# A two-block transformer on one core: filler transposes while TensorE waits at norms, block seams and router

## The reference

```python
def hybrid_layer(...):                      # first block, twice
    h = rmsnorm(x, norm1_w) * (1 + sc1) + sh1
    u = h @ w_in                            # 1024 x 5632
    ...                                     # pooling, short convolution, attention
    x = x + g1 * (merged @ w_out)
    h2 = rmsnorm(x, norm2_w) * (1 + sc2) + sh2
    x = x + g2 * ((silu(h2 @ w_gate) * (h2 @ w_up)) @ w_down)

def second_block(...):
    h = layer_norm(x, ln_in_g, ln_in_b)
    for l in range(2):
        mix = mixer_sublayer(h, ...)        # h @ w_in, 16 attention heads, @ w_out
        h = layer_norm(ALPHA * h + mix, ln1_g[l], ln1_b[l])
        scores = sigmoid(h @ router_w)      # 16 experts
        # best group of 4 experts, then the best 2 of its experts
        for e in range(16):
            y += gate[:, e] * ((silu(h @ w_gate[e]) * (h @ w_up[e])) @ w_down[e])
        h = layer_norm(ALPHA * h + y, ln2_g[l], ln2_b[l])
    return h
```

## Time and profile before

| | us |
|---|---|
| median of 3 runs (lowest, highest) | 1684.8 (1683.87, 1691.77) |
| the profiled execution, its own time | 1684.51 |
| its span, first to last instruction | 1682.7 |
| PE busy | 1567.5 (93% of the span) |
| DVE busy | 930.2 (55%) |
| ACT busy | 624.3 (37%) |
| weights moved | 427.66 MB, mean 254 GB/s |
| mean granted clock of PE | 0.966 of full |

### The profile page before, as it was taken

The page is one execution under the profiler, slowest core; times in us unless marked ns, Lnnn a source line. Parts: engine busy times, 40 slices in busy tenths (PEclk is TensorE's granted clock), DMA queues, the critical chain, the costliest instruction groups (busy, mean ns, idle before and its releaser), DMA issues.

```text
span 1682.7 us, 19021 instructions
## 1 busy us (share of the span) xinstructions
PE 1567.5 (93%) x7519; PEld 1072.6 (64%) x7519; DVE 930.2 (55%) x1401; ACT 624.3 (37%) x904; POOL 49.8 (3%) x66
## 2 busy tenths in 40 slices
PE   2899998999899998999989998999988999999996
PEld 2777787888778787788878774333336876433332
DVE  5888687865578978755467864111006786211002
ACT  2354544434344464444335742111114573111111
POOL 2000000000000000000030200000000110000000
PEclk8899999999999999999989998999998998999998
DMA  9677555976567734765565337999995417799995
GB/s 340 220 249 245 185 177 179 318 259 225 190 232 256 271 126 152 274 209 176 190 162 188 101 128 302 410 409 409 409 371 176 153 51 267 305 409 408 409 409 215
DMA packets 149980, 427.66 MB, mean 254 GB/s; under 512 B 8120, under 2 KB 16560, under 8 KB 149888
## 3 DMA queue, kind: packets, MB, share of 16 engines
q1 hardware_dynamic: 146208, 417.43, 67.8%
q0 software_dynamic: 3456, 8.87, 1.8%
q10 hardware_dynamic: 224, 0.07, 0.0%
HBM read 425.30 MB, written 1.05 MB: 253 GB/s over the span
## 4 chain that ended last, share of the span: by engine, by line
PE 62%; DVE 17%; DMA 7%; SPq 7%; ACT 4%; issue 3%; DVEq 0%; ACTq 0%
PE gp L2341 26%; PE gp L2788 9%; PE gp L2564 9%; SPq L756 6%; PE gp L2807 4%; DVE wlo L1424 4%; DMA raw<-in_w_in 3%; PE mp L2828 2%; DMA raw_deep<-in_exp_w_up 2%; PE gp L2773 2%; ACT whi L872 2%; DMA raw_deep<-in_w_ada 2%; DVE acc L1296 1%; DVE ft L1485 1%; PE mp L2625 1%
## 5 line engine op out<-in xcount | busy, mean ns | idle before, releaser
L1424 DVE TENSOR_TENSOR wlo<-raw,whi 128x2048 fp32r<-128x2048 f32 (+1 forms) x131 | 287.2, 2193 | 171.0 <-ACT whi L872 168.8
L872 ACT ACTIVATE whi<-raw 128x2048 fp32r<-128x2048 f32 (+1 forms) x131 | 240.0, 1835 | 297.3 <-PE gp L2341 162.7
L2341 PE MATMUL gp<-whi,xt_hi 128*128 128x512 f32 (+1 forms) x792 | 313.9, 396 | 16.7 <-DVE xt_lo L1495 7.4
L2341 PE MATMUL gp<-whi,xt_lo 128*128 128x512 f32 (+1 forms) x792 | 305.0, 385 | 0.0
L2341 PE MATMUL gp<-wlo,xt_hi 128*128 128x512 f32 (+1 forms) x792 | 304.7, 385 | 0.0
L2341 PEld LDWEIGHTS gp<-whi,xt_hi 128*128 128x128 f32 x792 | 151.0, 191 | 54.7 <-issue 14.4
L2341 PEld LDWEIGHTS gp<-whi,xt_lo 128*128 128x128 f32 x792 | 150.7, 190 | 30.2
L2341 PEld LDWEIGHTS gp<-wlo,xt_hi 128*128 128x128 f32 x792 | 151.0, 191 | 27.6 <-issue 1.0
L2196 DVE TENSOR_SCALAR pr<-slots,key,dg 128x128 f32<-128x128 f32 x64 | 19.3, 343 | 255.2 <-PE gp L2818 255.2
L1296 DVE SCALAR_TENSOR_TENSOR acc<-raw,cact,acc 128x1024 f32<-128x1024 f32 x69 | 88.5, 1282 | 2.6 <-DMA raw<-in_w_ada 1.1
L2210 DVE TENSOR_TENSOR pr<-pr,gp 64x512 f32<-64x512 f32 x32 | 21.7, 679 | 123.3 <-ACT pr L1214 123.3
(11 more groups left out here) (443 smaller groups left out, 2476.1 us busy)
## 6 DMA issues: line engine op xcount, KB each, us to landing
raw<-in_w_in SPq DMA_DIRECT2D x60, 1024.0 KB, 5.8
raw<-in_w_ada SPq DMA_DIRECT2D x42, 1024.0 KB, 5.3
raw_deep<-in_exp_w_gate SPq DMA_DIRECT2D x28, 1024.0 KB, 16.2
raw_deep<-in_exp_w_up SPq DMA_DIRECT2D x28, 1024.0 KB, 14.9
raw_deep<-in_exp_w_down SPq DMA_DIRECT2D x28, 1024.0 KB, 15.0
raw<-in_w_gate SPq DMA_DIRECT2D x20, 1024.0 KB, 5.1
raw<-in_w_up SPq DMA_DIRECT2D x20, 1024.0 KB, 5.2
raw<-in_w_down SPq DMA_DIRECT2D x20, 1024.0 KB, 5.0
```

Source lines behind the costliest of these rows:

```text
L872: act.activation(halves1(s, l, units, cols)[0], slot(raw, g % RAW, units, cols), ACT.Copy).then_inc(hi_done.sem, 1)
L1424: dve.tensor_tensor(lo, slot(raw, g % RAW, units, cols), hi.bitcast(F32), ALU.subtract).then_inc(raw_read[g % RAW].sem, 1)
L2341: mm = pe.matmul(gp[:, q % 2, t, 0:wide], a[:, chunk, ts], w[:, unit, c0:c0 + wide], start=first and n == 0 and m == 0, stop=last and n == ...
```

## The change

A helper, `keep_busy(bank, n)`, transposes the 128x128 identity n times into the first 128 columns of a PSUM bank that nothing reads. It is called at six places, 192 such transposes in all: 28 behind `turn_tile(0)` in `begin` (three calls), 40 ahead of the turn of tile 0 in layer 1 of the second block, 10 behind that turn in both layers, 8 behind `folded(0)` in both routers, and 16 ahead of the first gather in both. Where the bank is one of a dense pair, a wait for `pair_free` stands ahead; the product behind it has the same wait.

```diff
+            def keep_busy(bank, n):
+
+                for _ in range(n):
+                    pe.transpose(bank[:, 0:P], ident[:, :], ident[:, :])
...
                     pe.wait_ge(*xn_ready.at(l, xn0 + 1))
                     turn_tile(0)
+                    q = group_jobs(s0)[0][0]
+
+                    pe.wait_ge(*pair_free[q % 2].at(l, 2 * (q // 2)))
+                    keep_busy(gp[:, q % 2, 0, :], 28)
                     pe.wait_ge(*ft_lo.at(l, f0 + 1))
                     product(s0, (0,))
...
+                if l > 0:
+                    keep_busy(bank_xg, 40)
                 turn_tile(0)
+
+                pe.wait_ge(*pair_free[0].at2(l, 0))
+                keep_busy(gp[:, 0, 0, :], 10)
                 for s in range(2):
                     pe.wait_ge(*ft_lo.at2(l, X2_IN + s + 1))
                     product(s, (0,))
...
                 logits(0)
                 folded(0)
+                keep_busy(bank_gu, 8)
 
                 pe.wait_ge(*x2_sum.at2(l, 5))
...
                     if c == 0:
+                        if group == 0:
+                            keep_busy(bank, 16)
                         pe.wait_ge(*pick_ready.at2(l, NT * (group + 1)))
```

## The result

The changed kernel took 1697.6 us (median of 20 runs, 1687.3 to 1704.2), the kernel before, on the same chip, 1690.5 (20 runs, 1680.8 to 1694.0). The ratio is 1.0041, with a 95% interval of 1.0028 to 1.0054: about 7 us slower, where 0.8 us was forecast, and outside the range. Half of the miss is in the base: the 1684.5 us of before's profiled execution is near the low end of its runs.

The account below looks back on a forecast made before the run. PE was taken as busy nearly throughout but partly at half clock, with each stretch set by its last-ending chain; 1684.51 - 2.2 (layer 1) + 3.0 (routers) = 1685.3, stated as 1685.5 us, range 1679.5 to 1691.

Parts of the forecast that it names:

- Second block, layer 1: Start of layer 1's second block: fillers keep the clock full, unit 2's product starts earlier, all passed on: 2.2 us faster.
- The three calls of `begin`: At each `begin`: fillers fit PE's idle time, but the chain runs over DVE and ACT, so 0 gained.
- The routers: Both routers: fillers stand where PE is wanted, each 1.5 us slower, +3.0 for both.
- The two terms: In each router: +1.0 for the 8 behind `folded(0)`, +0.5 for the 16 ahead of the gather.
- one to one: Expert stage: bound by loading, its stream without a hole, so a router's delay of 1.5 us shifts it in full.
- lower bound of -1.8 for both: Both routers' best case, each with a full clock throughout; the 16 came to -0.2 if the clock is held.
- the first rival: Routers' fillers cost nothing net, the clock full and the gather warm: -4.0 in all, 1680.5 us; chance 0.2.
- Second block, layer 0: Start of layer 0's second block: DVE's chain sets the time, ten fillers end ahead of `wlo`; 0 gained.
- The gain stands alone: Layer 1's -2.2 kept and routers' fillers costing nothing net, -1.8: 1680.5 us; chance 0.2.
- The transposes don't hold the clock: By the skill's rule no stretch is held; layer 1 loses 1.7, each router 5.3: 1697 us; chance 0.07.
- The rises that I had argued from: Two clock rises behind eight transposes and some 512-wide matmuls, one in layer 1, taken to show that transposes hold the clock.
- All cold time comes back: PE sets the time at every seam, so 25.3 us come back: 1659.5 us; chance 0.04.

Follow-up runs that it names:

- the delays of 1.5 and 2.0 us: Kernel before plus transposes ahead of layer 1's second-block attention: 14 with untouched seam, 1.0041; 18 with the ten fillers in each seam, 0.9991.
- the 20: Kernel before plus 20 fillers ahead of the fourth head's value product of the first block, in each layer: 0.9974, again 0.9979.
- e3_router: Kernel before plus only the routers' fillers, 8 and 16 in each layer: 1.0023, or +3.9 us.
- e7_fourteen: The whole change with 14 fillers in place of the 40, timed against the kernel before: 1.0068.
- the 14: 14 fillers in place of the 40: 1.0068 in the otherwise whole change; 1.0013 with the routers' 8 and 16 out, 5 ahead of the flag wait.
- e2_seam: Kernel before plus only the second block's fillers, 10 in layer 0, 40 and 10 in layer 1: 1.0035, or +5.9 us.
- e5_forty: Kernel before plus only the 40 fillers ahead of layer 1's second-block turn of tile 0: 1.0009.

## Why the prediction was wrong

- **The base.** The step "The profiled execution lies 0.3 below the median of before" took the times of three runs for the kernel's. In the comparison the median was 1690.5, 5.7 us above the 1684.8 that I used. The repeats of before had spans of 1689.1 and 1687.3.
- **Second block, layer 1: the step that failed.** It failed twice. "40 fillers are 4.4 us at the full clock, which PE still has when they start; they end a microsecond ahead of the turn": they start 2.1 us late behind "issue" idle time, the clock is at half for 3.5 us of them, and they overran the turn by 2.7 us (20.1 us from that last expert matmul to the turn before, 22.8 after). The rest of the sum was right, and due to the ten: the tens alone shortened the seam by 2.2 us. With both it gained 0.8 to 1.1. Then "so all of it is passed on: -2.2 us" failed, and this is what the time shows: with the seam 2.2 us shorter, the tens alone were 3.2 and 4.1 us slower by their two ratios. Attention 1 behind them took 140.7 and 140.6 us, 4.3 more than before, and 141.0 in two of three profiles of the changed kernel. I had priced everything behind the seam as merely shifted. That is true only while the clock stays the same there, and the delays of 1.5 and 2.0 us show that it doesn't.
- **The three calls of `begin`: 0.** Right at the places named: the chain at the first is unmoved, PE waits longer for L1424 (0.89 us against 0.64), the clock holds (in six profiles with the 28s it was full at 14 of 18 calls, in the others at none). The 28s alone gave 1.0004. Further on, the first block's stage is 208.8 to 210.9 us in six profiles with the 28s, mean 209.7, and 203.7 to 210.3 in eleven without them or the 20, mean 207.5; the clock was at half at the wait named next for 6.8 to 10.2 us in all of the six and for 0 to 6.8 in the eleven. The wait for L1632 in it, whose cold matmuls follow, was 1.1 to 2.7 us with, 0 to 2.4 without. That a sooner `begin` sends PE sooner into this wait would fit, but the two ranges overlap and no experiment isolates it.
- **The routers: +3.0.** The two terms were mis-sized, the sum was near: luck, since the errors cancel. Eight fillers took 1.74 us up to the next row, 1.8 forecast. But from the router's turn to the flag five profiles with them (two layers each) average 16.0 us and eleven without 16.3: -0.3, not +1.0, in each router (single ones lie between 15.0 and 17.3 either way). The sixteen: load averages 12.1 us with them and 11.2 without, +0.9, not +0.5. The expert stage, which I had as shifted "one to one", is 214.6 us on average with them and 213.9 without: +0.7 more, by the late fall of the clock in four of ten. Together 1.3 for each router, 2.6 for both; by the timed runs of `e3_router` +3.9 (0.8 to 7.1). The prediction's lower bound of -1.8 for both doesn't follow from its own -0.2 for each, and the first rival's sum rests on it.
- **Second block, layer 0: 0.** The tens add nothing to the seam there (turn to turn 9.35 us before and after). Attention 0 behind it is long or short in either kernel.
- **The rivals.** *The gain stands alone* needed free routers: they aren't. *The transposes don't hold the clock* comes near in time (1697) and is wrong in cause: in the changed kernel's first profile the clock is 1.00 through all three `begin`s. The rule of the Trainium skill (TensorE: Matmul & The Clock Gate, Part 4: PE-mode transpose), that the full clock does not engage for transposes, is not borne out by these fp32 transposes: 28 ran at 0.11 us each, and in the 40 the clock rose from half to full among nothing but fillers. The rises that I had argued from held 512-wide matmuls too and proved less. *All cold time comes back*: the page's clock did rise, and the time with it.

Seam -0.9, attention 1 +3.2, routers +2.6 and first block +2.2 (means of the profiles named) come to the measured +7.1. That they meet proves nothing. The sum leaves out attention 0 (+2.4 by the same means), the first block's share is argued only, and the spans of the three profiles of each kernel differ by 11.4 us on average. What the runs show is that attention 1 and the routers each cost some 3 us; how the rest divides is open.

## What to carry to other kernels

A filler in one wait can change where the clock falls 70 us later, so its gain at the wait is not its worth: profile each kernel more than once, and compare stages, not spans. Where two stage lengths alternate between executions, ask which the profile at hand shows before taking it as the base. Size fillers to the wait less the "issue" idle time ahead of them (here about 2 us), and put none ahead of a wait that is about to end; that alone did not make this kernel faster (`e7_fourteen`).

## What was not expected of the hardware

- In an attention of short matmuls (64 to 256 columns) TensorE lost its full clock behind 4 us in which it was recorded busy for 3.83. In before it was busy for the same 3.83 us there and for 3.52 of the next 4, and kept the clock. With the loss it did 72 matmuls in 15 us, without it 108.
- Whether it did went with the instant: 1.5 us later brought the loss, 2.0 us more behind another seam removed it.
- The expert stage took 1.7 us more where a fall of the clock came 10 us ahead of its end, six times of 40, than where it came 24 us ahead of it.
- Fillers at the seam came behind 1.9 to 2.2 us of "issue" idle time in every profile that has the 40 or the 14, and long runs of them had 1.3 to 2.3 us more in their midst in two (`e2_seam`, `e5_forty`). What causes it no run here shows.
